# Expert weights of an MoE decoder step: where the gate and up halves land in their slot, and which queue issues the down weights

## What is computed

```
x = normed tokens                                   # 320 x 1024
scores = sigmoid(x @ router_w)                      # 64 experts, each token picks 8
gates  = normalised scores of the 8 picked, times 2.5
hid    = silu(x @ exp_w_gate[e]) * (x @ exp_w_up[e])    # 1024 x 256 each
routed = sum over e of (hid * gates[e]) @ exp_w_down[e] # 256 x 1024
shared = (silu(x @ shared_w_gate) * (x @ shared_w_up)) @ shared_w_down
x = x + g_f * (routed + shared), then a final norm
```

## Time and profile before

| | |
|---|---|
| median of 3 runs | 993.21 us |
| the runs | 984.48, 993.21, 999.41 us |
| span of the profiled execution | 998.1 us |
| nearest run time to it | 999.41 us, 1.3 us more than the span |
| PE busy | 798.7 us (80%) |
| DVE, ACT, POOL busy | 393.9, 235.7, 306.1 us |
| moved by DMA | 277.75 MB, mean 278 GB/s |
| packets under 2 KB | 154931 of 192230 |
| SP's ring q1 | 250.88 MB; POOL's q0 22.57 MB; ACT's q10 2.76 MB |

### The profile page before, as it was taken

One profiled execution on the slowest core, in us unless ns is written; L12 is line 12 of the kernel. 1 busy time (PEld: TensorE's weight loads), 2 busy tenths in 40 slices (PEclk: granted clock), 3 DMA queues, 4 the chain that ended last, 5 costly groups with the idle time before them and its releaser, 6 DMA issues.

```text
span 998.1 us, 16529 instructions
## 1 busy us (share of the span) xinstructions
PE 798.7 (80%) x5564; PEld 449.7 (45%) x5565; DVE 393.9 (39%) x825; ACT 235.7 (24%) x405; POOL 306.1 (31%) x285
## 2 busy tenths in 40 slices
PE   1979999999888799876796888888788788887910
PEld 1657555445444355443443444444444344443500
DVE  2235183656144643233342343334334334444306
ACT  2112543023132222122121221222122122222202
POOL 0120000021133444344334343433334434344323
PEclk8879999999897889878888889887888988988965
DMA  9977846345689999989998999899899989999234
GB/s 273 398 244 240 304 164 231 117 149 212 226 251 362 367 318 334 324 251 348 311 316 287 315 316 327 252 349 310 281 340 321 360 285 334 358 331 353 68 58 145
DMA packets 192230, 277.75 MB, mean 278 GB/s; under 512 B 20355, under 2 KB 154931, under 8 KB 183548
## 3 DMA queue, kind: packets, MB, share of 16 engines
q1 hardware_dynamic: 165654, 250.88, 72.3%
q0 software_dynamic: 21216, 22.57, 10.2%
q10 hardware_dynamic: 5254, 2.76, 1.1%
HBM read 270.14 MB, written 25.89 MB: 297 GB/s over the span
## 4 chain that ended last, share of the span: by engine, by line
PE 54%; DMA 26%; issue 10%; DVE 6%; POOL 1%; POOLq 1%; ACT 1%; SPq 1%; DVEq 0%
DMA et<-xn_rows,idx 16%; PE bank L1049 15%; PE bank L1085 12%; DMA acc_rows<-et,idx 5%; PE bank L770 4%; PE bank L778 3%; PE bank L1032 3%; PE bank L913 3%; PE bank L797 2%; DMA gu<-in_ada_w 2%; PE bank L755 2%; DMA small<-halfc 2%; PE bank L1009 1%; PE bank L1136 1%; PE bank L781 1%
## 5 line engine op out<-in xcount | busy, mean ns | idle before, releaser
L1049 PE MATMUL bank<-gu,et 128*64 128x256 f32 x2496 | 295.9, 394 | 33.3 <-issue 31.0
L1049 PEld LDWEIGHTS bank<-gu,et 128*64 128x64 f32 x2496 | 185.6, 144 | 168.2 <-issue 91.4
L1085 PE MATMUL bank<-dn,et 128*64 128x512 f32 x624 | 183.5, 726 | 2.3 <-DVE et L1534 1.2
L449 POOL DMA_INDIRECT acc_rows<-et,idx x64 | 105.6, 1649 | 226.1 <-DVE et L1541 164.1
L430 POOL DMA_INDIRECT et<-xn_rows,idx x64 | 80.8, 1263 | 193.9 <-DVE idx L1516 133.7
L1534 DVE COPY et<-bank 128x256 f32<-128x256 f32 x64 | 27.1, 424 | 222.8 <-PE bank L1066 218.6
L690 ACT ACTIVATE et<-bank 64x512 f32<-64x512 f32 x64 | 37.8, 590 | 265.9 <-PE bank L1049 263.1
L1032 PE MATMUL bank<-ident,et 128*128 128x128 f32 x256 | 50.0, 328 | 62.3 <-DMA et<-xn_rows,idx 35.6
L1085 PEld LDWEIGHTS bank<-dn,et 128*64 128x64 f32 x624 | 46.6, 163 | 88.7 <-issue 88.7
L1520 DVE COPY et<-bank 128x512 f32<-128x512 f32 x64 | 44.3, 692 | 103.5 <-PE bank L1032 99.9
L1541 DVE TENSOR_SCALAR et<-bank,pick_out 128x512 f32<-128x512 f32 x64 | 48.1, 751 | 81.4 <-PE bank L1085 76.5
(11 more groups left out here) (269 smaller groups left out, 684.0 us busy)
## 6 DMA issues: line engine op xcount, KB each, us to landing
gu<-in_exp_w_gate SPq DMA_DIRECT2D x64, 1024.0 KB
gu<-in_exp_w_up SPq DMA_DIRECT2D x64, 1024.0 KB
dn<-in_exp_w_down SPq DMA_DIRECT2D x64, 1024.0 KB
gu<-in_ada_w SPq DMA_DIRECT2D x12, 2048.0 KB, 13.9
gu<-in_w_in SPq DMA_DIRECT2D x4, 2048.0 KB, 19.5
gu<-in_w_out SPq DMA_DIRECT2D x2, 2048.0 KB, 13.1
acc_rows<-dn SPq DMA_DIRECT2D x2, 1280.0 KB, 16.2
small<-halfc POOLq DMA_DIRECT2D x100, 0.0 KB
```

The source lines that it names most:

```text
L449: pool.indirect_dma_start(acc_rows[0], bass.IndirectOffsetOnAxis(ap=idx[:, u, 0:1], axis=0), yo[:, u % 2, 0, :], None, bounds_check=2 * T ...
L1049: mm = pe.matmul(bank[u % 2][64 * c:64 * c + 64, b * FE:(b + 1) * FE], xt[:, b, k % 4, k // 4, :], w[:, k, c * FE:(c + 1) * FE], start=(k ...
L1085: mm = pe.matmul(bank[5 + b][64 * c:64 * c + 64, :], hT[:, b, j, :], dn[:, dslot(u), j * D + c * HALF:j * D + (c + 1) * HALF], start=(j == ...
```

## The change

The HBM views of the gate and up weights are flattened to one run per partition. The slot is read as two halves of 2048 values per partition: gate in the first, up in the second (`halves`); the products read it through `pair`, which finds the 256 values of row k at half c. So both DMAs write 8 KiB per partition in one run. The shared expert's gate and up weights do the same; their products get a function of their own, since the two halves of a 512-wide operand now lie 2048 values apart. The down weights of the experts leave SyncE's queue: ScalarE issues the first three after line 643, the others in each slot after `y1`, for the expert three ahead. Their wait is for the same count of `y_ready` as before.

```
-        eg = io["exp_w_gate"][0].rearrange("e (p k) f -> e p k f", k=KT)
-        eu = io["exp_w_up"][0].rearrange("e (p k) f -> e p k f", k=KT)
+        eg = io["exp_w_gate"][0].rearrange("e (p k) f -> e p (k f)", k=KT)
+        eu = io["exp_w_up"][0].rearrange("e (p k) f -> e p (k f)", k=KT)
...
+        def halves(slot):
+            return gu[slot][:, :, :].rearrange("p k n -> p (k n)").rearrange("p (c m) -> p c m", c=2)
+        def pair(slot):
+            return halves(slot).rearrange("p c (k f) -> p c k f", k=KT)
...
             for c, name in enumerate(("shared_w_gate", "shared_w_up")):
-                sync.dma_start(gu[SH_SLOT][:, :, c * FE:(c + 1) * FE],
-                               io[name][0].rearrange("(p k) f -> p k f", k=KT)).then_inc(ld_shared_gu, 16)
+                sync.dma_start(halves(SH_SLOT)[:, c, :],
+                               io[name][0].rearrange("(p k) f -> p (k f)", k=KT)).then_inc(ld_shared_gu, 16)
...
-                sync.dma_start(gu[gslot(u)][:, :, 0:FE], eg[e]).then_inc(ld_gu[gslot(u)], 16)
-                sync.dma_start(gu[gslot(u)][:, :, FE:2 * FE], eu[e]).then_inc(ld_gu[gslot(u)], 16)
-
-            def load_dn(r, i, u):
...
-                sync.dma_start(dn[:, dslot(u), :], ed[i * U + u]).then_inc(ld_dn[dslot(u)], 16)
+                sync.dma_start(halves(gslot(u))[:, 0, :], eg[e]).then_inc(ld_gu[gslot(u)], 16)
+                sync.dma_start(halves(gslot(u))[:, 1, :], eu[e]).then_inc(ld_gu[gslot(u)], 16)
...
             with sync.Fori(1, NE // U) as i:
                 for u in range(U):
                     load_gu(0, i, u)
-                    load_dn(0, *back(i, u))
...
+            act.wait_ge(s["ya_done"], CT)
+            act.wait_ge(s["mix_free"], 1)
+            for u in range(3):
+                act.dma_start(dn[:, dslot(u), :], ed[u]).then_inc(ld_dn[dslot(u)], 16)
...
+            def load_dn(r, i, u):
+                g = r * NE + i * U + u
+                if isinstance(g, int) and g == SLOTS - 1:
+                    act.wait_ge(s["sh_down_ready"], 5)
+                elif not (isinstance(g, int) and g < SLOTS):
+                    act.wait_ge(s["y_ready"], g - (SLOTS - 1))
+                act.dma_start(dn[:, dslot(u), :], ed[i * U + u]).then_inc(ld_dn[dslot(u)], 16)
...
                     if not (first and u == 0):
                         y1(r, i if u else i - 1, (u - 1) % U)
+                    if not (last and u >= U - 3):
+                        load_dn(r, i + (u + 3) // U, (u + 3) % U)
...
+            def shared_product(t, ks):
+                t0, n = TILES[t]
+                w = pair(SH_SLOT)
+                for k in ks:
+                    if t < 2:
+                        mm = pe.matmul(bank[4 + t][:, :].rearrange("p (c f) -> p c f", c=2), xT[:, k, t0:t0 + n], w[:, :, k, :],
+                                       start=(k == 0), stop=(k == KT - 1))
+                    else:
+                        for c in range(2):
+                            mm = pe.matmul(bank[4 + t][64 * c:64 * c + 64, 0:FE], xT[:, k, t0:t0 + n], w[:, c, k, :],
+                                           start=(k == 0), stop=(k == KT - 1))
+                return mm
...
-                w = gu[gslot(u)]
+                w = pair(gslot(u))
...
-                                           w[:, k, c * FE:(c + 1) * FE], start=(k == 0), stop=(k == KT - 1))
+                                           w[:, c, k, :], start=(k == 0), stop=(k == KT - 1))
```

More of the change, by code:

```diff
@@ L306, in load_gu @@
                 e = i * U + u
-                sync.dma_start(gu[gslot(u)][:, :, 0:FE], eg[e]).then_inc(ld_gu[gslot(u)], 16)
-                sync.dma_start(gu[gslot(u)][:, :, FE:2 * FE], eu[e]).then_inc(ld_gu[gslot(u)], 16)
-            def load_dn(r, i, u):
[L311 to L315, removed]
-                sync.dma_start(dn[:, dslot(u), :], ed[i * U + u]).then_inc(ld_dn[dslot(u)], 16)
-            def back(i, u):
-                return (i, u - 1) if u else (i - 1, U - 1)
+                sync.dma_start(halves(gslot(u))[:, 0, :], eg[e]).then_inc(ld_gu[gslot(u)], 16)
+                sync.dma_start(halves(gslot(u))[:, 1, :], eu[e]).then_inc(ld_gu[gslot(u)], 16)
             for u in range(3):
@@ L325, in _ @@
             sync.dma_start(dn[:, 0, :], io["shared_w_down"][0].rearrange("(p j) n -> p (j n)", j=2)).then_inc(ld_shared_dn, 16)
[L326 to L331, removed]
+            for u in range(3, U):
                 load_gu(0, 0, u)
-                load_dn(0, 0, u - 2)
-            load_dn(0, 0, U - 2)
             with sync.Fori(1, NE // U) as i:
@@ L337, in _ @@
                     load_gu(0, i, u)
-                    load_dn(0, *back(i, u))
-            load_dn(0, NE // U - 1, U - 1)
             sync.wait_ge(s["flags"], 1)
@@ L345, in _ @@
                         load_gu(r, 0, u)
-                        if u:
-                            load_dn(r, 0, u - 1)
                     with sync.Fori(1, NE // U) as i:
@@ L350, in _ @@
                             load_gu(r, i, u)
-                            load_dn(r, *back(i, u))
-                    load_dn(r, NE // U - 1, U - 1)
             sync.wait_ge(s["routed"], 1)
@@ L710, in body @@
                         y1(r, i if u else i - 1, (u - 1) % U)
+                    if not (last and u >= U - 3):
+                        load_dn(r, i + (u + 3) // U, (u + 3) % U)
             def rounds(r):
+                if r:
+                    for u in range(3):
+                        load_dn(r, 0, u)
                 xt1(r, 0, 0)
@@ L945, in _ @@
             wout(2, range(4, KT))
-            def shared_gu(t):
-                tile_product(bank[4 + t], t, gu[SH_SLOT], 2 * FE).then_inc(s["sh_ready"], 1)
+            def shared_product(t, ks):
[10 more added lines that the diff above has]
+                return mm
             def logits(t):
@@ L962, in _ @@
             pe.wait_ge(ld_shared_gu, 32)
-            tile_product(bank[4], 0, gu[SH_SLOT], 2 * FE, range(4))
+            shared_product(0, range(4))
             turn("z", "xn_ready", 1)
-            tile_product(bank[4], 0, gu[SH_SLOT], 2 * FE, range(4, KT)).then_inc(s["sh_ready"], 1)
+            shared_product(0, range(4, KT)).then_inc(s["sh_ready"], 1)
             pe.wait_ge(s["tp_evac"], TP["z11"] + 1)
@@ L981, in _ @@
             spread_gf(3)
-            tile_product(bank[5], 1, gu[SH_SLOT], 2 * FE, range(4))
+            shared_product(1, range(4))
             pe.wait_ge(s["mask_done"], 1)
@@ L995, in _ @@
             mm.then_inc(s["tp_ready"], 1)
-            tile_product(bank[5], 1, gu[SH_SLOT], 2 * FE, range(4, KT)).then_inc(s["sh_ready"], 1)
+            shared_product(1, range(4, KT)).then_inc(s["sh_ready"], 1)
             def pick(r, i, u):
@@ L1152, in rounds @@
                     pe.wait_ge(s["gf_in"], 6)
-                    shared_gu(2)
+                    shared_product(2, range(KT)).then_inc(s["sh_ready"], 1)
                 pick(r, 0, 1)
```

## The result

The changed kernel takes 1033.62 us (median of 4 runs, 1029.66 to 1037.87), beside 994.6 us for the kernel before on the same chip: ratio 1.042, 95% interval 1.034 to 1.050. It is 4.2% slower; 950 us, 4.3% faster, was forecast. Its profiled execution spans 1035.6 us, 37.5 more than before.

A forecast was written before the change was run, and what follows sets the result against it. Bound: latency of small DMAs (gathers) behind weight bursts. Waits -30, clock -18, back edge -8, turns +13 make -43: 999.4 to 956 us, median 6.2 lower, so 950; own range 925 to 972, 8-in-10 range 905 to 1003.

The forecast's parts named there:

- ScalarE's issue: Down-weight issue on ScalarE after y1: 0.33 us, covered by 2.7 us before the next `gates`, cost 0.
- the products' new order: Matrix products: same matmuls and columns in another order of address, 0; shared expert's split columns between 0 and 1 us.
- How much earlier a gather lands: Waits at turn_x: each gather lands 1.2 us sooner, 25 waits, -30 us in all; bounds 0 and 3.6 us each.
- The start of service: Gather's delay from issue to first packet: 3.6 us behind 8 KiB packets against 5.0 behind 1 KiB, 1.4 less.
- the burst drains 1.1 us sooner: Gate and up loads in each slot: 4.9 us instead of 6.0 at the higher rate of 8 KiB packets.
- the clock's -18: PE clock after shorter waits at turn_x: 9 slots regain 2 us each, -18 us; bounds 0 and 55.
- the back edge's -8: Seven stalls at the hardware loop's back edge, entry and exit: 1.2 us less each, -8 us; range 0 to -31.
- slower turns: Gather's service among 8 KiB packets: 1.6 us more in 8 of 25 waits, +13 us; between 0 and 58.
- The nine turns of a gather: Gather's service: 128 rows over 16 engines and a semaphore write each make 9 turns, each alternating with a foreign packet.
- The down weights' move: Down loads from SyncE's to ScalarE's queue: 0 for itself; effect on gathers left to the second rival.
- the second rival: At turn_x, three loaded rings with big packets slow gathers: waits +38 us, clock 11 more, 1042 us; chance 0.13.
- overlap for 1 to 3 us only: Argument against the second rival: down is issued about 3.5 us after gate and up, which need 4.9.

The follow-up runs named there:

- the eighth of the bytes: The changed kernel with only an eighth of each expert's gate, up and down weights loaded, same issues and queues: 861.8 us, ratio 0.869 to the kernel before.
- e1: The kernel before with only the gate and up layout changed to 8 KiB packets, down weights still on SyncE's queue: 1011.3 us, ratio 1.017.
- e2: The changed kernel with gate and up back in 1 KiB runs, so only the down weights' move to ScalarE's queue remains: 1024.5 us, ratio 1.032.
- 2 + 2 KiB: The kernel before with gate and up and down weights all in 2 KiB packets, all on SyncE's queue: 968.9 us, ratio 0.975.

## Why the prediction was wrong

**The bound was read rightly.** The waits at turn_x are for gathers, and they carry the time: the eighth of the bytes takes 75.5 us of waits, 50.0 of busy time and 11.6 at the back edge off the kernel before, 137.1 of 137.7 us. Also right: 21811 packets under 2 KB; ScalarE's issue, 0.34 us for the 0.33 forecast, and hidden; SyncE's long issues gone (1.3 us at most now, 5.9 before); the products' new order, 0 (e1's account closes without it); the tail and the start of the program. The reading of the bound had one gap, the scatter ahead of the gather in the same ring (below).

**The step that failed is "How much earlier a gather lands", 25 x 1.2 = -30 us in the sum.** It had two parts. The start of service was to come 1.4 us sooner behind 8 KiB packets, on one write (3.6 against 5.0 us). For gathers with a clear ring it came 0.6 us sooner with the whole change (18 of the same 18) and 0.5 with the layout alone (17 of 17), so the sign was right and the size less than half. The other part, that the burst drains 1.1 us sooner, is true of the burst, but the step took either gain for a gain in landing, and in each of 25 waits. The gather is served beside the weights, a turn at a time, as rows 12 said, and the turns took back what the start gave: of the gathers of first blocks, sorted by the kernel before, the 24 with a clear ring landed after 7.3 us before and 7.2 after, and the 37 behind another DMA of their own ring after 6.7 us before and 8.7 after. The prediction had no term for that second place: it priced every gather as if it were alone in q0. Why the queue costs there is argued from the turns, each packet ahead in q0 paying foreign ones of its own; no run alters that queue alone. With this step gone, the clock's -18 and the back edge's -8 had nothing to stand on: busy time rose by 4.2 us, and the back edge gave 3.1.

**The term "slower turns", +13, was mis-sized.** It took 8 waits of 25 at 1.6 us. What was measured is 28 waits at 4.1 us against 25 at 3.1, 35.8 us more. By the halves the layout cost 10.6 us of waits, and the third ring the other 25. That the 10.6 lie near the 13 is luck: they are the sum of about -2.5 and +13.4 in two places, and the step before had promised -30 beside them. The nine turns of a gather were seven, too: rows 9 show a whole gather in 112 packets over 16 engines.

**The down weights' move, priced 0 for itself, was the larger half** (+3.2% alone). The text left its effect on gathers to the second rival and gave that 0.13. The rival had the place and the sign, and its sum came out: 38 us more of waits and 1042 us forecast, 35.8 and 1033.6 measured. In part that is luck, since it spread 1.5 us evenly over 25 waits, where 12 gathers behind their own ring brought 32.5 of the 35.8 us. Against it stood that the down load and gate and up "overlap for 1 to 3 us only". The window at 320.4 shows them together for 4.2 us, all of one gather's service: the overlap is short, but the gather is issued into it, in the same part of every slot. A chance should follow where in the slot the overlap lies, not how long it is.

## What to carry to other kernels

Before making descriptors of bulk loads longer, or giving them a second ring, look whether a small DMA of another ring is on the critical path, and what stands ahead of it in its own ring: on one ring of 8 KiB packets each packet of the small DMAs went with one foreign packet, and a second loaded ring added to that. Here 2 KiB for all of the bulk gave 2.5% where 8 KiB cost 1.7% on one ring and 4.2% on two, though the DMA share fell in each case. When a wait is for latency, a better rate elsewhere is no argument; and when the small DMAs are made earlier, look at what else stands in their queue (here scatters that wait for scatters): the best kernel, 2 KiB packets and lists one expert earlier, is 6.7% faster than before.

## What the hardware showed that I had not expected

- A gather's first packet comes 4.2 to 5.1 us after its issue (medians, own ring clear) where weights are in flight at full rate, and 1.7 to 2.0 us when little is. Longer packets of gate and up make it sooner: 5.0 us with 1 KiB, 4.3 with 8. What fills the difference to 2 us stayed open.
- While a gather is served, each of its packets goes with one foreign packet of 8 KiB (101 against 102), but with more foreign packets the shorter they are, over the whole window: 102 against 168 at 4 KiB, 100 against 231 at 2, 106 against 347 at 1.
- The second hardware ring cost the kernel 22 to 25 us where packets of 8 KiB were among the weights; with 2 KiB packets the medians are 15 us apart, in two comparisons.
- TensorE's busy time does not follow the waits in proportion: 10.6, 24.9 and 35.8 us more of waits cost 5.5, 1.2 and 4.2 us of it (e1, e2, after; mean granted clock 0.879, 0.883, 0.872), 19.2 us less gave 10.5 back (2 + 2 KiB, 0.909), and 75.5 us less, where nearly all waits had gone, gave 50.0 (0.951).
